# Three transformer layers on one core: x, the normalised x and the gated product at other SBUF addresses

## The chip, the core and the metric

The kernel runs on one core of a Trainium2 chip. The metric is the device time of one execution in microseconds (us), the median of the runs of a kernel. A profiled execution gives one trace: for every instruction its engine, start and length. PE is the matrix engine (TensorE), PEld its weight loads; DVE, ACT and POOL are the vector, scalar and GpSimd engines; SP only issues DMAs here.

## What is computed

Three layers over 256 tokens of width 1024, batch 1, float32 throughout: layer A (three dilated attentions of 16 heads), layer B (block attention of 16 heads) and layer C (attention of 8 heads with a forget gate, a convolution and a pooling branch), each followed by the same kind of gated MLP with a short causal convolution. Cut to the MLP, which the change names:

```python
def conv_ffn(h, w_up, conv_w, conv_b, w_down):
    u = h @ w_up                                     # 1024 -> 2 x 2816
    up = jnp.pad(u, ((0, 0), (CONV_WIDTH - 1, 0), (0, 0)))
    uc = conv_b + sum(conv_w[j] * up[:, j:j + S] for j in range(CONV_WIDTH))
    gate, val = uc[..., :D_FF], uc[..., D_FF:]
    return (jax.nn.silu(gate) * val) @ w_down        # 2816 -> 1024
```

## The kernel before

**Precision.** Every large product is made of three fp32r matmuls. A weight chunk arrives in `w_raw` by DMA; ACT copies it rounded into `w_hi` (L362), and DVE subtracts to get the rest, `w_lo` (L370). The activations are split alike: the normalised x into `xg` (for each of 8 blocks k of 128 channels, 256 tokens of the high part and then 256 of the low part), the attention's output into `mix_hi` and `mix_lo`, the MLP's gated product into `g_hi[b]` and `g_lo[b]` (two buffers each, b = 0, 1). hi·hi, hi·lo and lo·hi are summed in PSUM.

**Weight stream.** 372 chunks of up to 1024 columns pass through a ring of six buffers for each of `w_raw`, `w_hi` and `w_lo`. All waits are semaphores written by hand, and every engine runs its instructions in the order of the code.

**The stages on PE.** Each layer has

- attention (`unit_chunk_pe`): `xg` is the stationary operand (128 columns of a block), the weights move, 384 columns a matmul, lines L650, L651 and L652. The small matmuls of scores, transposes and values lie between them;
- the output projection (`out_pe`): a weight tile is stationary and `mix_hi` or `mix_lo` moves, 256 columns, lines L1189, L1190, L1191, eight times the three for a chunk;
- the MLP (`ffn_pe`), 24 steps j = 0 to 23. A step with j < 22 has two chunks of the up projection (`project2`): for each of eight blocks k one matmul of 512 columns, `w_hi` stationary and high and low part of `xg` moving (L402), then one of 256 columns, `w_lo` stationary and the high part moving (L404). A step with j > 1 then has one chunk of the down projection: for each of eight tiles m three matmuls of 256 columns, with a weight tile stationary and `g_hi[j % 2]` or `g_lo[j % 2]` moving (L1707, L1708, L1709). Steps 4 to 19 run in a loop of eight turns with two steps each. The up projection writes PSUM banks 0 and 1 in even steps, 2 and 3 in odd ones; the down projection adds into banks 4 to 7 throughout.

Layer C has six further chunks ahead of its attention (`project_k`, L388 to L390): weight stationary, `xg` moving, 256 columns, three matmuls for a block.

**Addresses.** SBUF tensors lie one behind the other in the order of the code, each on a multiple of 32 bytes. Addresses below are bytes within a partition; a float is 4 bytes, a 128-column slice 512 bytes, a 256-column one 1024. `x_all` holds 16 gains of the first norm in its first 64 bytes and x behind them (`xT`); `norm_gain` (called by ACT and DVE) reads the gains there for the first norm, and `load_x` on SP fills both.

Of the kernel before, what the change touches and what calls it, by code (L numbers as in the profile page):

```python
# [8 lines left out]
P = 128  # L9
D = 1024  # L10
TOK = 256
KT = D // P
# [27 lines left out]
WARM_UP = 16  # L40
HALVES = 3
GAINS = 16
CHUNK = KT * P
UNIT = 3 * P
QCHUNK = 2 * UNIT
# [112 lines left out]
def build(nc, x_d, xa_d, stream_d, par_d, con_d, taps_d, out_d):  # L158
# [7 lines left out]
    def sb(name, shape, dt=F32):  # L166
        return nc.alloc_sbuf_tensor(name, shape, dt)
# [5 lines left out]
    w_raw = [sb(f"w_raw{s}", [P, CHUNK]) for s in range(RING)]  # L173
    w_hi = [sb(f"w_hi{s}", [P, CHUNK], F32R) for s in range(RING)]
    w_lo = [sb(f"w_lo{s}", [P, CHUNK], F32R) for s in range(RING)]
    x_all = sb("x_all", [P, GAINS + KT * TOK])
    xT = x_all[:, GAINS:GAINS + KT * TOK].rearrange("p (k t) -> p k t", t=TOK)
    xg = sb("xg", [P, KT, 2, TOK], F32R)
    xg_hi, xg_lo = xg[:, :, 0, :], xg[:, :, 1, :]
    mix_hi = sb("mix_hi", [P, KT, TOK], F32R)  # L180
# [1 line left out]
    par = sb("par", [P, N_PAR])  # L182
    con = sb("con", [P, N_CON])
    zero = sb("zero", [P, TOK], BF16)
    ln_x = sb("ln_x", [P, TOK])
    rms_r = sb("rms_r", [P, TOK])

# [248 lines left out]
    def norm_gain(e, m):  # L436

        g = PAR_NORM + KT * e + m
        return x_all[:, m:m + 1] if e == 0 else par[:, g:g + 1]

    def first_hi_dve(eng):
        eng.wait_ge(x_first, 16)
# [1612 lines left out]
    with nc.Block() as block:  # L2055

        @block.sync
        def _(sp):
            def load(c):
                s, w = c % RING, chunk_cols(c)  # L2060
                sp.dma_start(w_raw[s][:, 0:w], stream_d[c, :, 0:w]).then_inc(w_loaded[s], 16)


            def load_half(c, kk):
                part = slice(kk * UNIT, (kk + 1) * UNIT)
                sp.dma_start(w_raw[c][:, part], stream_d[c, :, part]).then_inc(half_in[c] if kk == 0 else w_loaded[c], 16)

            def load_x(m, n, landed):
                part = slice(GAINS + m * TOK if m else 0, GAINS + (m + n) * TOK)
                sp.dma_start(x_all[:, part], xa_d[:, part]).then_inc(landed, 16)  # L2070

            load_x(0, 1, x_first)
            load_x(1, 1, x_in[0])
            for kk in range(2):
                load_half(1, kk)
            load_x(2, 2, x_in[1])
            for kk in range(2):
                load_half(2, kk)
            load(3)
            load_x(4, 2, x_in[2])  # L2080
            load(4)
            load(5)
            load_x(6, 2, x_in[3])
            sp.dma_start(con[:, 0:CON_MASKA], con_d[:, 0:CON_MASKA]).then_inc(con_in, 16)
            sp.dma_start(par[:, 0:PAR_FFN], par_d[:, 0:PAR_FFN]).then_inc(row_in, 16)
            for c in range(RING, N_CHUNKS):
                sp.wait_ge(w_lo_done, c - RING + 1)
                load(c)
                if c == RING + 10:
                    sp.dma_start(con[:, CON_MASKA:], con_d[:, CON_MASKA:]).then_inc(rest_in, 16)  # L2090
                if c == A_OUT:
                    sp.wait_ge(rest_in, 16)
                    sp.dma_start(par[:, PAR_FFN:], par_d[:, PAR_FFN:]).then_inc(rest_in, 16)
                if c == A_FFN:
                    sp.dma_start(taps[:], taps_d[:, :]).then_inc(taps_in, 16)
                if c == RING + 16:
                    sp.wait_ge(x_lo, KT)
                    sp.wait_ge(x_sq, KT)
                    for q in range(UCH):
                        sp.dma_start(xT[:, 2 * q:2 * q + 2], x_d[2 * q:2 * q + 2].rearrange("k p t -> p k t")).then_inc(x_in[q], 16)  # L2100
            for m in range(0, KT, 2):
                sp.wait_ge(x_new, 5 * KT + m + 1)
                sp.dma_start(out_d[m], xT[:, m, :]).then_inc(stored, 16)
            sp.wait_ge(stored, 16 * KT)

        @block.tensor
        def _(pe):

            pe.wait_ge(warm, 1)
            for n in range(WARM_UP):  # L2110
                nc.tensor.matmul(bank(7), zero[:, 0:P], zero[:], start=True, stop=True, skip_group_check=True)
            att_a_pe(pe)
            ffn_stage(pe, 0, ffn_pe(0))
            att_b_pe(pe)
            ffn_stage(pe, 1, ffn_pe(1))
            pre_pe(pe)
            att_c_pe(pe)
            ffn_stage(pe, 2, ffn_pe(2))

        @block.scalar  # L2120
        def _(act):
            for kk, landed in ((0, half_in[0]), (1, w_loaded[0])):
                part = slice(kk * UNIT, (kk + 1) * UNIT)
                act.dma_start(w_raw[0][:, part], stream_d[0, :, part]).then_inc(landed, 16)
            nc.scalar.preload_act_table_set("natural_log_exp_and_others")
            half_split_hi(act, 0, 0)
            half_split_hi(act, 0, 1)
            resid_act(act, 0, 1)
            half_split_hi(act, 1, 0)
            half_split_hi(act, 1, 1)  # L2130
            resid_act_sq(act, 0)
            resid_act_sq(act, 1)
            resid_act(act, 0, 2)
            half_split_hi(act, 2, 0)
            resid_act(act, 0, 3)
            half_split_hi(act, 2, 1)
            split_hi(act, 3)
            resid_act(act, 0, 4)
            resid_act(act, 0, 5)
            split_hi(act, 4)  # L2140
            split_hi(act, 5)
            resid_act(act, 0, 6)
            resid_act(act, 0, 7)
            resid_act_sq(act, 2)
            resid_act_sq(act, 3)
            att_a_act(act)
            ffn_stage(act, 0, ffn_act(0))
            nc.scalar.preload_act_table_set("natural_log_exp_and_others")
            end_act(act, 2)
            att_b_act(act)  # L2150
            ffn_stage(act, 1, ffn_act(1))
            nc.scalar.preload_act_table_set("natural_log_exp_and_others")
            end_act(act, 4)
            pre_act_f(act)
            att_c_act(act)
            ffn_stage(act, 2, ffn_act(2))
            for m in range(1, KT, 2):
                act.wait_ge(x_new, 5 * KT + m + 1)
                act.dma_start(out_d[m], xT[:, m, :]).then_inc(stored, 16)

        @block.vector
        def _(dve):
            nc.vector.memset(zero[:], 0.0).then_inc(warm, 1)
            first_hi_dve(dve)
            half_split_lo(dve, 0, 0)
            resid_dve_lo(dve, 0, 0)
            half_split_lo(dve, 0, 1)
            resid_dve_lo(dve, 0, 1)
            half_split_lo(dve, 1, 0)
            half_split_lo(dve, 1, 1)  # L2170
            resid_dve_lo(dve, 0, 2)
            half_split_lo(dve, 2, 0)
            resid_dve_lo(dve, 0, 3)
            half_split_lo(dve, 2, 1)
            split_lo(dve, 3)
            resid_dve_lo(dve, 0, 4)
            resid_dve_lo(dve, 0, 5)
            split_lo(dve, 4)
            split_lo(dve, 5)
            resid_dve_lo(dve, 0, 6)  # L2180
            resid_dve_lo(dve, 0, 7)
            gains_dve(dve)
            att_a_dve(dve)
            ffn_stage(dve, 0, ffn_dve(0))
            end_dve(dve, 2, acc, B_QKV)
            att_b_dve(dve)
            ffn_stage(dve, 1, ffn_dve(1))
            end_dve(dve, 4, acc, C_PRE)
            pre_dve_f(dve)
            att_c_dve(dve)  # L2190
            ffn_stage(dve, 2, ffn_dve(2))
            end_dve(dve, 6, acc, N_CHUNKS)

        @block.gpsimd
        def _(pool):
            nc.gpsimd.memset(cv_h[0][:], 0.0).then_inc(zeroed, 1)
            nc.gpsimd.memset(cv_h[1][:], 0.0).then_inc(zeroed, 1)
            resid_pool(pool, 0)
            tables_pool(pool)
            att_a_pool(pool)  # L2200
            resid_pool(pool, 1)
            ffn_stage(pool, 0, ffn_pool(0))
            resid_pool(pool, 2)
            att_b_pool(pool)
            resid_pool(pool, 3)
            ffn_stage(pool, 1, ffn_pool(1))
            resid_pool(pool, 4)
            pool_zeroes(pool)
            pre_pool_f(pool)
            resid_pool(pool, 5)  # L2210
            ffn_stage(pool, 2, ffn_pool(2))
# [62 lines left out]
def first_input(w):  # L2274

    x = np.zeros((P, GAINS + KT * TOK), np.float32)
    x[:, 0:KT] = w["attn_norm"][0].reshape(KT, P).T
    x[:, GAINS:] = w["x"][0].T[:, class_order()].reshape(KT, P, TOK).transpose(1, 0, 2).reshape(P, KT * TOK)
    return x
# [87 lines left out]
```

## Time and profile before

| | |
|---|---|
| median of 3 runs | 1060.22 us (1059.83 to 1062.07) |
| the profiled execution | 1060.19 us |
| its span, first to last instruction | 1058.4 us |
| PE busy | 1053.8 us, 7508 matmuls |
| PE weight loads busy | 981.7 us |
| DVE / ACT / POOL busy | 862.2 / 685.9 / 342.0 us |
| granted TensorE clock | 1.00 throughout |

The profile models the end of a matmul, and neighbours overlap in it: the length of one matmul (281 ns for 256 columns) isn't what it costs. The cost is the distance from its start to the next one's start. So the timeline is read here by starts: the start of a chunk's first matmul, subtracted from that of the next chunk.

### The profile page before, as it was taken

The page shows a single profiled execution, that of the slowest core. Times are in us where ns is not written, and L with a number is a line of the kernel's source. Part 1 is how long each engine was busy: PE and PEld are TensorE (multiplying, and loading weights), DVE is VectorE, ACT ScalarE, POOL GpSimd, SP SyncE. Part 2 cuts the span into 40 slices and gives each one's busy share as a digit, 9 for nine tenths or more (in the row PEclk, how much of TensorE's full clock was granted, in tenths as well). Part 3 has the DMA queues.
Part 4 walks back from the last instruction along what each step waited for, and adds up shares of the span by engine and source line. Part 5 has one row for each costly group of instructions (what it writes and reads, how often), then busy time and mean ns, then how long its engine had stood idle before and what let it go on. Part 6 is the DMA issues. An engine that isn't in the chain of part 4 may idle for free.

```text
span 1058.4 us, 21208 instructions
## 1 busy us (share of the span) xinstructions
PE 1053.8 (100%) x7508; PEld 981.7 (93%) x7508; DVE 862.2 (81%) x1588; ACT 685.9 (65%) x1262; POOL 342.0 (32%) x368
## 2 busy tenths in 40 slices
PE   9999999999999999999999999999999999999998
PEld 8999999999999999999989899999998999999998
DVE  7877778877799888887777998888896769988886
ACT  7766676776766555576776665555686666655552
POOL 4312222121365333322122553333350025533331
PEclk9999999999999999999999999999999999999999
DMA  9644545455466555535453675555434436655541
GB/s 317 225 159 150 164 151 180 149 185 196 161 219 198 195 181 190 159 110 179 152 164 120 216 216 187 188 187 189 134 112 144 146 114 225 212 187 190 183 154 41
DMA packets 57749, 183.34 MB, mean 173 GB/s; under 512 B 6352, under 2 KB 9680, under 8 KB 57424
## 3 DMA queue, kind: packets, MB, share of 16 engines
q1 hardware_dynamic: 56816, 181.52, 52.7%
q8 instruction: 41, 0.67, 0.3%
q10 hardware_dynamic: 864, 0.92, 0.3%
q14 instruction: 28, 0.23, 0.1%
HBM read 181.36 MB, written 1.05 MB: 172 GB/s over the span
## 4 chain that ended last, share of the span: by engine, by line
PE 99%; DMA 0%; DVE 0%; ACT 0%; DVEq 0%; issue 0%
PE ps L402 23%; PE ps L404 12%; PE ps L650 10%; PE ps L652 9%; PE ps L651 9%; PE ps L1707 6%; PE ps L1709 6%; PE ps L1708 6%; PE ps L1189 2%; PE ps L1191 2%; PE ps L1190 2%; PE ps L584 1%; PE ps L809 1%; PE ps L854 1%; PE ps L783 1%; PE ps L821 1%
## 5 line engine op out<-in xcount | busy, mean ns | idle before, releaser
L370 DVE TENSOR_TENSOR w_lo<-w_raw,w_hi 128x1024 fp32r<-128x1024 f32 (+2 forms) x369 | 441.0, 1210 | 56.0 <-ACT w_hi L362 55.3
L362 ACT ACTIVATE w_hi<-w_raw 128x1024 fp32r<-128x1024 f32 (+2 forms) x369 | 354.1, 972 | 163.3 <-PE ps L404 136.6
L402 PE MATMUL ps<-xg,w_hi 128*128 128x512 f32 x1056 | 374.7, 396 | 0.0
L404 PE MATMUL ps<-xg,w_lo 128*128 128x256 f32 x1056 | 297.0, 281 | 0.0
L402 PEld LDWEIGHTS ps<-xg,w_hi 128*128 128x128 f32 x1056 | 198.6, 188 | 44.6
L404 PEld LDWEIGHTS ps<-xg,w_lo 128*128 128x128 f32 x1056 | 198.1, 188 | 0.1
L1829 POOL TENSOR_TENSOR prob_t<-prob_t,qkT 128x256 f32<-128x256 f32 x63 | 100.3, 1593 | 289.6 <-ACT prob_t L1752 289.6
L650 PE MATMUL ps<-w_hi,xg 128*128 128x384 f32 (+1 forms) x556 | 193.1, 347 | 0.0
L652 PE MATMUL ps<-w_hi,xg 128*128 128x384 f32 (+1 forms) x556 | 186.8, 336 | 0.0
L651 PE MATMUL ps<-w_lo,xg 128*128 128x384 f32 (+1 forms) x556 | 186.7, 336 | 0.0
L1707 PE MATMUL ps<-g_hi,w_hi 128*128 128x256 f32 x528 | 149.2, 283 | 0.0
L1709 PE MATMUL ps<-g_hi,w_lo 128*128 128x256 f32 x528 | 148.9, 282 | 0.0
L1708 PE MATMUL ps<-g_lo,w_hi 128*128 128x256 f32 x528 | 148.6, 281 | 0.0
L1823 POOL TENSOR_TENSOR qkT<-prob,rms_r 128x256 f32<-128x256 f32 x132 | 119.2, 922 | 19.0 <-DVE prob L1766 10.3
L1799 DVE SCALAR_TENSOR_TENSOR qkT<-qkT,par 128x255 f32<-128x255 f32 (+1 forms) x264 | 111.6, 476 | 4.3 <-ACT qkT L1745 4.2
L650 PEld LDWEIGHTS ps<-w_hi,xg 128*128 128x128 f32 x556 | 104.4, 188 | 3.4 <-issue 2.7
L651 PEld LDWEIGHTS ps<-w_lo,xg 128*128 128x128 f32 x556 | 104.5, 188 | 0.1
L652 PEld LDWEIGHTS ps<-w_hi,xg 128*128 128x128 f32 x556 | 104.3, 188 | 0.0
L1707 PEld LDWEIGHTS ps<-g_hi,w_hi 128*128 128x128 f32 x528 | 99.6, 189 | 2.7
L1745 ACT ACTIVATE qkT<-qkT,par 128x256 f32<-128x256 f32 x132 | 76.4, 597 | 37.6 <-POOL qkT L1823 37.4
L1708 PEld LDWEIGHTS ps<-g_lo,w_hi 128*128 128x128 f32 x528 | 99.7, 189 | 0.0
L1709 PEld LDWEIGHTS ps<-g_hi,w_lo 128*128 128x128 f32 x528 | 99.3, 188 | 0.0
(182 smaller groups left out, 1388.5 us busy)
## 6 DMA issues: line engine op xcount, KB each, us to landing
w_raw<-w_stream SPq DMA_DIRECT2D x228, 512.0 KB, 3.6
w_raw<-w_stream SPq DMA_DIRECT2D x137, 384.0 KB, 3.4
w_raw<-w_stream SPq DMA_DIRECT2D x4, 392.0 KB, 3.0
con<-consts SPq DMA_DIRECT2D x1, 1024.0 KB, 7.5
x_all<-x_t SPq DMA_DIRECT2D x4, 256.0 KB, 5.5
conv_taps<-taps SPq DMA_DIRECT2D x1, 1024.0 KB, 7.1
w_raw<-w_stream SPq DMA_DIRECT2D x4, 192.0 KB, 4.4
x_all<-x_a SPq DMA_DIRECT2D x3, 256.0 KB, 5.5
```

What stands on the lines that cost most here:

```text
L362: nc.scalar.activation(w_hi[s][:, 0:w], w_raw[s][:, 0:w], ACT.Copy).then_inc(w_hi_done, 1)
L370: nc.vector.tensor_tensor(w_lo[s][:, 0:w], w_raw[s][:, 0:w], w_hi[s][:, 0:w].bitcast(F32), ALU.subtract).then_inc(w_lo_done, 1)
L402: nc.tensor.matmul(bank(b, 0, 2 * TOK), w_hi[s][:, k * P:(k + 1) * P], xg[:, k, :, :].rearrange("p h t -> p (h t)"), start=(k == 0), stop= ...
L404: last = nc.tensor.matmul(bank(b), w_lo[s][:, k * P:(k + 1) * P], xg_hi[:, k, :], start=False, stop=(k == KT - 1), skip_group_check=True)
L650: nc.tensor.matmul(out, hi, wh, start=(k == 0), stop=False)
L651: nc.tensor.matmul(out, hi, wl, start=False, stop=False)
L652: last = nc.tensor.matmul(out, lo, wh, start=False, stop=(k == KT - 1))
L1707: nc.tensor.matmul(acc(m), wh, g_hi[b][:], start=first, stop=False, skip_group_check=True)
L1708: nc.tensor.matmul(acc(m), wh, g_lo[b][:], start=False, stop=False, skip_group_check=True)
L1709: last = nc.tensor.matmul(acc(m), wl, g_hi[b][:], start=False, stop=True, skip_group_check=True)
L1799: nc.vector.scalar_tensor_tensor(cv_s[b][s][:, k:TOK], up_s[b][s][:, 0:TOK - k], par_col(f, t, per, i, 4 * s + 2 - k), cv_s[b][s][:, k:TOK ...
L1823: nc.gpsimd.tensor_tensor(up_s[t % 2][s], up_sum[s], rms_r[:], ALU.mult).then_inc(F.up, 1)
```

## The change

Only where tensors lie in SBUF changes. `X0` = 256 floats now stand ahead of x in `x_all`, and the gains occupy the last 16 of them; so x's split between gains and data falls 1024 bytes into `x_all` in place of 64 bytes. An unused tensor `gap` of 176 floats is put behind `zero`. Instructions, their order on every engine, their waits and the sizes of the transfers stay as they are.

| tensor | address before, modulo 1024 (128) | after, modulo 1024 (128) |
|---|---|---|
| w_raw, w_hi, w_lo, slice k | 128 + 512k (0) | the same |
| x (`xT`) | 192 (64) | 128 (0) |
| xg, high and low part of each block | 192 (64) | 128 (0) |
| mix_hi, mix_lo | 192 (64) | 128 (0) |
| con | 64 (64) | 0 (0) |
| ln_x, rms_r, tokbuf, qkT, v_tok, prob0, prob_t | 96 (96) | 736 (96) |
| g_hi, g_lo, both buffers | 256 (0) | 896 (0) |

```diff
+X0 = TOK
+GAP = 176
...
-    x_all = sb("x_all", [P, GAINS + KT * TOK])
-    xT = x_all[:, GAINS:GAINS + KT * TOK].rearrange("p (k t) -> p k t", t=TOK)
+    x_all = sb("x_all", [P, X0 + KT * TOK])
+    xT = x_all[:, X0:X0 + KT * TOK].rearrange("p (k t) -> p k t", t=TOK)
...
     zero = sb("zero", [P, TOK], BF16)
+    sb("gap", [P, GAP])
     ln_x = sb("ln_x", [P, TOK])
...
-        return x_all[:, m:m + 1] if e == 0 else par[:, g:g + 1]
+        return x_all[:, X0 - GAINS + m:X0 - GAINS + m + 1] if e == 0 else par[:, g:g + 1]
...
-                part = slice(GAINS + m * TOK if m else 0, GAINS + (m + n) * TOK)
-                sp.dma_start(x_all[:, part], xa_d[:, part]).then_inc(landed, 16)
+                a, b = GAINS + m * TOK if m else 0, GAINS + (m + n) * TOK
+                sp.dma_start(x_all[:, X0 - GAINS + a:X0 - GAINS + b], xa_d[:, a:b]).then_inc(landed, 16)
```

## Rows read from the trace of the kernel before

**Rows 1.** The page: span, engines' busy us, the granted TensorE clock.
```profile
span 1058.4 us, 21208 instructions
PE 1053.8 (100%) x7508; PEld 981.7 (93%) x7508; DVE 862.2 (81%) x1588; ACT 685.9 (65%) x1262; POOL 342.0 (32%) x368
PEclk9999999999999999999999999999999999999999
```
**Rows 2.** The page's chain that ended last, shares of the span.
```profile
PE 99%; DMA 0%; DVE 0%; ACT 0%; DVEq 0%; issue 0%
```
**Rows 3.** Waits of PE: waiter <- releaser: us in total, times, longest.
```profile
PE ps L2111 <- DVE zero L2163: 1.1, 1, 1.1
PE ps L584 <- ACT w_hi L377: 0.4, 1, 0.4
```
**Rows 4.** Matmuls by line: names, array, shape, count | busy us, mean ns | idle before.
```profile
L402 PE MATMUL ps<-xg,w_hi 128*128 128x512 f32 x1056 | 374.7, 396 | 0.0
L404 PE MATMUL ps<-xg,w_lo 128*128 128x256 f32 x1056 | 297.0, 281 | 0.0
L650 PE MATMUL ps<-w_hi,xg 128*128 128x384 f32 x540 | 187.5, 347 | 0.0
L1707 PE MATMUL ps<-g_hi,w_hi 128*128 128x256 f32 x528 | 149.2, 283 | 0.0
L1189 PE MATMUL ps<-mix_hi,w_hi 128*128 128x256 f32 x192 | 55.5, 289 | 0.0
```
**Rows 5.** Timeline, layer A's MLP: first matmuls of chunks (start us, us, matmul).
```profile
347.58 0.40 PE L402 MATMUL ps<-xg,w_hi 128*128 128x512 f32 x1
...
353.17 0.28 PE L1707 MATMUL ps<-g_hi,w_hi 128*128 128x256 f32 x1
...
356.01 0.40 PE L402 MATMUL ps<-xg,w_hi 128*128 128x512 f32 x1
...
361.67 0.28 PE L1707 MATMUL ps<-g_hi,w_hi 128*128 128x256 f32 x1
...
364.55 0.40 PE L402 MATMUL ps<-xg,w_hi 128*128 128x512 f32 x1
```
**Rows 6.** Timeline, layer B's output projection: first matmuls, 24 apart in each pair.
```profile
564.17 0.28 PE L1189 MATMUL ps<-mix_hi,w_hi 128*128 128x256 f32 x1
...
566.89 0.28 PE L1189 MATMUL ps<-mix_hi,w_hi 128*128 128x256 f32 x1
...
573.13 0.28 PE L1189 MATMUL ps<-mix_hi,w_hi 128*128 128x256 f32 x1
...
575.96 0.28 PE L1189 MATMUL ps<-mix_hi,w_hi 128*128 128x256 f32 x1
```
**Rows 7.** Timeline, attention: starts 12 matmuls apart, in layers A and B.
```profile
43.38 0.34 PE L650 MATMUL ps<-w_hi,xg 128*128 128x384 f32 x1
...
45.45 0.34 PE L650 MATMUL ps<-w_hi,xg 128*128 128x384 f32 x1
...
476.59 0.34 PE L650 MATMUL ps<-w_hi,xg 128*128 128x384 f32 x1
...
478.71 0.34 PE L650 MATMUL ps<-w_hi,xg 128*128 128x384 f32 x1
```
**Rows 8.** Timeline, layer B's first MLP chunk, and the next two pairs behind.
```profile
577.37 0.39 PE L402 MATMUL ps<-xg,w_hi 128*128 128x512 f32 x1
...
580.16 0.40 PE L402 MATMUL ps<-xg,w_hi 128*128 128x512 f32 x1
...
581.21 0.47 PE L402 MATMUL ps<-xg,w_hi 128*128 128x512 f32 x1
581.52 0.28 PE L404 MATMUL ps<-xg,w_lo 128*128 128x256 f32 x1
```
**Rows 9.** The page: groups of DVE and ACT, and a DMA issue.
```profile
L370 DVE TENSOR_TENSOR w_lo<-w_raw,w_hi 128x1024 fp32r<-128x1024 f32 (+2 forms) x369 | 441.0, 1210 | 56.0 <-ACT w_hi L362 55.3
x_all<-x_a SPq DMA_DIRECT2D x3, 256.0 KB, 5.5
```

## The prediction

> **What bounds the kernel now.** I read the page first. PE is busy for 1053.8 of 1058.4 us and the clock is granted in full in every slice [rows 1]; the chain that ended last is 99% PE [rows 2]; and PE's waits on other engines sum to 1.5 us, all at the start [rows 3]. DVE, ACT and POOL have room: DVE's largest group alone sits idle for 56.0 us, mostly waiting for ACT, which itself works ahead of PE [rows 9]. So the time is a sum over 7508 matmuls of the distance from one start to the next, and the change can matter only through these distances.
>
> They aren't N columns divided by 2.4 GHz. The timeline gives them: in layer A's MLP two up chunks (16 pairs of L402 and L404) take 353.17 - 347.58 = 5.59 us and the next two 361.67 - 356.01 = 5.66; one down chunk (24 matmuls of 256 columns) takes 2.84 us from 353.17 and the next 2.88 us from 361.67 [rows 5]. At 2.4 GHz 24 x 256 columns alone would be 2.56 us. So each chunk carries 9 to 12% that no wait accounts for, and the amount has two values for the same instructions. The timeline repeats this in all three MLPs: of 132 up chunks 62 go at half of 5.59 and 70 at half of 5.66; of 66 down chunks the 30 of the even steps up to j = 20 take 2.88 and the other 36 take 2.84 to 2.85.
>
> Two more rows say what kind of thing this is. The output projection has the same instructions as the down projection, with `mix` moving in place of `g`: its 24 matmuls take 2.72 us at one place and 2.83 at another [rows 6]. Attention's twelve matmuls of 384 columns take 2.07 us, or 2.12 [rows 7]. A pattern holds until something disturbs it: layer B's first MLP chunk goes at 2.79 us for eight pairs, has a hitch (0.31 us from an L402 to its L404, about 0.08 more than elsewhere) [rows 8], and goes in the slower pattern behind it. The pace is a state of PE's two operand streams, the weight loads and the moving reads, which lock to one another; addresses could have a part in which locks there are.
>
> **The change, part by part.**
>
> *Work and order.* Nothing is added or removed: the rows of PE, DVE, ACT, POOL and SP are the same in the same order with the same waits. Cost 0.
>
> *Other engines.* `w_raw`, `w_hi` and `w_lo` stay where they are, so the 441.0 us of DVE's split [rows 9] keep their addresses. What moves is x, xg, the attention's buffers and g. If these instructions got slower, PE's cover is the weight ring: it has waited for nobody since the start [rows 3]. x's first transfers land on other addresses, 64 bytes further within 128. That is ahead of the first matmul; the three large ones take 5.5 us to land [rows 9] for the same bytes. I take 0, with 0.1 us either way.
>
> *The down projection* (L1707 to L1709, 1584 matmuls; one line's 528 in [rows 4]). `g` goes from 256 to 896 modulo 1024, on a multiple of 128 both times. Here only the distance to the stationary weights changes: they start at 128 or 640, so g starts 128 behind one of them before and 256 behind one after. Bounds, from the nearest rows with these instructions: 2.72 us a chunk below [rows 6], 2.88 above [rows 5]. I take 2.83, the commoner pattern of the output projection, since the long runs of chunks there keep to it. The sum: 30 x (2.88 - 2.83) = 1.5, and 36 x 0.01 = 0.4: **-1.9 us**. The bounds are 30 x 0.16 + 36 x 0.12 = 9.1 us less, and 36 x 0.035 = 1.3 us more.
>
> *The up projection* (L402, L404, 1056 each [rows 4]). `xg` moves from 64 past a multiple of 128 onto one, and its distance to the weights falls from 64 to 0. The trace shows two patterns that take turns with the down projection's: a 2.88 chunk is followed by fast up chunks, a 2.84 chunk by slow ones [rows 5]. If the down projection settles in one pattern, the turns should end. The steps would then all be fast (70 chunks x 0.035 = 2.45 us less) or all slow (62 x 0.035 = 2.2 us more). I take fast, **-2.45 us**: after the 2.83 pattern of the output projection, layer B's MLP began with 2.79 for eight pairs, which is the fast one [rows 8]. The step leans on one place and is the weakest of the sum.
>
> *Attention and output projection.* `xg` is stationary there and moves by the same 64 bytes; the moving weights stay. 92 of 139 twelves are in the 2.07 pattern, the rest higher. All of them at 2.12 would be 92 x 0.05 = 4.6 us more, all at 2.07 some 2 us less. I see no reason for either and take 0.
>
> The sum is -1.9 - 2.45 = -4.35 us. The profiled execution took 1060.19 us, the median is 1060.22, so both give **1055.8 us**.
>
> **What the skill says.** The trace shows a cost that isn't in the column count (2.84 against 2.56 us [rows 5]) and differs for the same instruction. The Trainium skill, TensorE: Matmul & The Clock Gate, Step-by-step, says that PE has two independent SBUF read ports, so that loading the next weights takes nothing from the running matmul; its section Back-to-back issue gap has N/2.4 + 2.5 ns. By that 24 matmuls of 256 columns would take about 2.62 us (an estimate from that page), wherever they lie. The trace doesn't bear the figure out, in any pattern. SBUF — State Buffer of the same skill, Specifications, has cachelines of 16 bytes; all operands start on one before and after. By both pages the change would do nothing, which is the first rival.
>
> **The rivals.**
>
> 1. *Addresses of this kind don't matter.* Both patterns occur in one stage with the same addresses (up chunks at 5.59 and 5.66 [rows 5]), so what chooses between them is history, and the new addresses only redraw it to the same mix. For it: `xg`, off 128, and `g`, on 128, differ by little. Time: 1060.2. Chance 0.20.
> 2. *A deeper lock.* The new distances let the MLP lock where the output projection did for some chunks. The down chunks at 2.72 are 9.1 us less; the up projection at the rate per column of attention's 2.07 (2.07 / 12 / 384 = 0.449 ns) takes 16 x 768 x 0.449 ns = 5.52 us in place of a mean of 5.625, times 66 steps 6.9 us less: 1044.2, or 1051 if it is the down projection alone. Against it: no MLP chunk of the trace shows that lock. Chance 0.14.
> 3. *Slower: what lies on 128 goes slowest.* Of the moving operands of 256 columns the one on a multiple of 128, `g`, is the slowest in the trace (2.84 to 2.88), and `mix`, 64 off, is faster (2.72 to 2.83) [rows 5, 6]. If that is due to the multiple of 128, `xg` joins it. The place is the up projection. With every MLP chunk in the slower of its own two patterns the price is 2.2 + 1.3 = 3.5 us, 1063.7. At g's rate per column (2.88 / 24 / 256 = 0.469 ns) a step's 16 pairs would take 5.76 us, up to 8.9 us more. It decides as soon as more than half of the up steps fall into the slow pattern with nothing gained in the down projection. Against it: moving weights lie on 128 too, and attention has a good pattern with them (2.07 [rows 7]). Chance 0.28.
>
> **How the numbers follow.** The forecast, 1055.8, has 0.38; the deeper lock 0.14; nothing 0.20; slower 0.28. A measurement of this kernel can tell about 0.2%, 2.1 us, from no change: faster 0.38 + 0.14 = 0.52, the same 0.20, slower 0.28. The range reaches from the full deeper lock, 1044, past rival 3's price with part of attention's 4.6 us, to 1065. About 0.04 lie below and 0.09 above. Cases of both signs hold most of it; the forecast's own range is 1053 to 1058 (one of its two terms missing, or part of the deeper lock).
>
> **What would show it.** In the trace after, down chunks of 24 matmuls at 2.83 us or under, where 2.88 and 2.84 took turns; pairs of up chunks at 5.59 without turns; attention's twelves at 2.07 as before; PE still waiting for nobody. Down chunks still at 2.84 to 2.88 refute the first term, up chunks at 5.66 the second. If all starts are spaced as before, rival 1 holds; if starts are unchanged and the time isn't, then something outside PE's streams (a wait, a transfer at the start) does it, and the whole reading is wrong.

## The result

The changed kernel takes 1063.44 us (median of 19 runs, 1063.17 to 1063.70), the kernel before 1060.08 us on the same chip: a ratio of 1.0025, 95% interval 1.0018 to 1.0033. It is slower, by 3.4 us, where 4.4 us less were forecast.

The page of the changed kernel, span, busy times and clock, to be held against [rows 1]:

```profile
span 1061.7 us, 21208 instructions
PE 1056.7 (100%) x7508; PEld 982.6 (93%) x7508; DVE 862.1 (81%) x1588; ACT 685.8 (65%) x1262; POOL 339.0 (32%) x368
PEclk9999999999999999999999999999999999999999
```

Its chain and PE's waits (as [rows 2, 3]):

```profile
PE 97%; DVE 1%; DMA 1%; SPq 1%; ACT 0%; POOL 0%; issue 0%; DVEq 0%; POOLq 0%
```
```profile
PE ps L2114 <- DVE zero L2166: 1.1, 1, 1.1
PE ps L587 <- ACT w_hi L380: 0.5, 1, 0.5
PE ps L700 <- POOL tokbuf L1162: 0.3, 1, 0.3
```

PE waits for others for 1.9 us in place of 1.5, at full clock. The rest of the 3.3 us of span is in the distances from one matmul's start to the next. The timeline of layer A's MLP after the change, first matmuls of chunks, answers to [rows 5] (lines are 3 further down in the file: L1710 was L1707, L405 was L402, L1192 was L1189):

```profile
353.77 0.28 PE L1710 MATMUL ps<-g_hi,w_hi 128*128 128x256 f32 x1
...
356.64 0.40 PE L405 MATMUL ps<-xg,w_hi 128*128 128x512 f32 x1
...
362.29 0.28 PE L1710 MATMUL ps<-g_hi,w_hi 128*128 128x256 f32 x1
...
365.18 0.40 PE L405 MATMUL ps<-xg,w_hi 128*128 128x512 f32 x1
```

Down chunks take 2.87 and 2.89 us; they took 2.84 and 2.88. A pair of up chunks takes 5.65, and from step 3 on every such pair does, where 5.59 and 5.66 took turns. And the output projection of layer B, 24 matmuls from start to start, where [rows 6] had 2.72 and 2.83:

```profile
573.12 0.28 PE L1192 MATMUL ps<-mix_hi,w_hi 128*128 128x256 f32 x1
...
576.00 0.28 PE L1192 MATMUL ps<-mix_hi,w_hi 128*128 128x256 f32 x1
```

2.88 us, that is 120.0 ns a matmul.

The table below is what all experiments are read by. It sums, over a whole trace, the distance from each matmul's start to the next one's, by the stage of the first. "D" is the distance in bytes from the start of the stationary weight tile to the start of the moving operand, modulo 512 (a tile is 512 bytes wide, so every tile of a chunk looks the same); the changed kernel's g starts 768 bytes behind the weights' start, so its D is 256. In attention the roles are turned, xg being the stationary operand; it is listed under the same D of xg. A chunk's ns a matmul, or a pair, is its time to the next chunk's start divided by its 24 matmuls, or its 8 pairs.

| kernel | D of xg, mix, g | median us | attention | output proj. | up | down |
|---|---|---|---|---|---|---|
| before | 64, 64, 128 | 1060.1 | 298.7 | 70.0 | 372.1 | 188.5 |
| changed | 0, 0, 256 | 1063.4 | 298.9 | 71.4 | 372.8 | 189.9 |
| e1_x_only | 0, 0, 128 | 1061.8 | 298.7 | 71.4 | 372.7 | 188.1 |
| e2_g_only | 64, 64, 256 | 1058.3 | 301.1 | 70.1 | 370.0 | 189.0 |
| e3_g_64 | 64, 64, 192 | 1057.4 | 301.2 | 70.1 | 373.9 | 179.9 |
| e4_all_64_on | 0, 0, 256 | 1063.5 | 298.5 | 71.4 | 372.8 | 189.9 |
| e5_all_192 | 192, 192, 192 | 1057.0 | 297.7 | 68.8 | 373.8 | 186.4 |
| e6_g_320_448 | 64, 64, 320 and 448 | 1058.4 | 298.6 | 70.0 | 373.6 | 184.8 |
| e7_g_64_96 | 64, 64, 64 and 96 | 1061.2 | 298.7 | 70.0 | 373.7 | 187.9 |
| e8_x_448_g_192 | 448, 448, 192 | 1057.0 | 298.0 | 68.8 | 373.8 | 186.4 |
| e9_x_192_g_64 | 192, 192, 64 | 1056.5 | 298.0 | 68.8 | 373.0 | 186.5 |
| e10_weights_alone | 0, 0, 64 | 1055.6 | 298.7 | 71.4 | 369.5 | 185.8 |
| e11_x_320_g_448 | 320, 320, 448 | 1056.0 | 298.7 | 70.0 | 373.6 | 182.0 |
| e12_x_0_mix_192_g_192 | 0, 192, 192 | 1047.0 | 298.1 | 68.8 | 368.3 | 180.9 |
| e13_x_0_mix_192_g_64 | 0, 192, 64 | 1052.7 | 297.6 | 68.8 | 369.8 | 185.6 |
| e14_gap_32 | 0, 0, 192 | 1049.7 | 299.4 | 71.4 | 367.8 | 180.8 |

Attention has two values where xg is at D = 64. In the trace of the kernel before most twelves of layer A are at 2.07 us; in those of e2_g_only and e3_g_64, with the same addresses there, most are near 2.12 (176.5 ns a matmul). Layer A's attention takes 196.0 us in the first and 198.5 in the other two; layers B and C differ by 0.1 at most. That fits the runs of the kernel before, which lie in two groups, near 1060.0 and 1062.2. The profiled execution of e2_g_only had the dearer attention and lies above the median (1061.12 against 1058.33 us). That of e3_g_64 had it too, and is still the fastest of its seven (1055.94, median 1057.35), so its other executions lost more in some other stage: one trace isn't the median in every stage. The other stages are compared from the traces, the whole by medians and intervals.

### The profile page after: what moved, and what is told of

It reads as the page before. It is cut to its first block, busy times and chain, and to the rows that moved or that the text cites. A ratio compares the mean times of both kernels' runs of the same rounds, so it can differ in the third digit from the quotient of the medians.

```text
span 1061.7 us, 21208 instructions
## 1 busy us (share of the span) xinstructions
PE 1056.7 (100%) x7508; PEld 982.6 (93%) x7508; DVE 862.1 (81%) x1588; ACT 685.8 (65%) x1262; POOL 339.0 (32%) x368
## 4 chain that ended last, share of the span: by engine, by line
PE 97%; DVE 1%; DMA 1%; SPq 1%; ACT 0%; POOL 0%; issue 0%; DVEq 0%; POOLq 0%
PE ps L405 23%; PE ps L407 12%; PE ps L653 9%; PE ps L655 9%; PE ps L654 9%; PE ps L1712 6%; PE ps L1711 6%; PE ps L1710 6%; PE ps L1192 2%; PE ps L1193 2%; PE ps L1194 2%; PE ps L812 1%; PE ps L857 1%; PE ps L786 1%; PE ps L824 1%; PE ps L843 1%
## 5 line engine op out<-in xcount | busy, mean ns | idle before, releaser
L405 PE MATMUL ps<-xg,w_hi 128*128 128x512 f32 x1056 | 375.5, 398 | 0.0
L405 PEld LDWEIGHTS ps<-xg,w_hi 128*128 128x128 f32 x1056 | 198.5, 188 | 46.0
L655 PE MATMUL ps<-w_hi,xg 128*128 128x384 f32 (+1 forms) x556 | 186.5, 336 | 0.0
L1710 PE MATMUL ps<-g_hi,w_hi 128*128 128x256 f32 x528 | 149.4, 283 | 0.0
L1826 POOL TENSOR_TENSOR qkT<-prob,rms_r 128x256 f32<-128x256 f32 x132 | 116.3, 899 | 19.2 <-ACT rms_r L518 7.0
L1710 PEld LDWEIGHTS ps<-g_hi,w_hi 128*128 128x128 f32 x528 | 100.3, 190 | 2.9
```

Source lines behind the costliest of these rows:

```text
L405: nc.tensor.matmul(bank(b, 0, 2 * TOK), w_hi[s][:, k * P:(k + 1) * P], xg[:, k, :, :].rearrange("p h t -> p (h t)"), start=(k == 0), stop= ...
L655: last = nc.tensor.matmul(out, lo, wh, start=False, stop=(k == KT - 1))
L1710: nc.tensor.matmul(acc(m), wh, g_hi[b][:], start=first, stop=False, skip_group_check=True)
L1826: nc.gpsimd.tensor_tensor(up_s[t % 2][s], up_sum[s], rms_r[:], ALU.mult).then_inc(F.up, 1)
```

## The experiments

The first question was which of the moved things costs the time, and whether a tile's own address or its distance to the weights does it.

**x alone, g alone.**

```diff
# e1_x_only: the change's lines for x with X0 = 256, and
+    sb("gap", [P, 16])
# e2_g_only: only, ahead of g_hi,
+    sb("gap_g", [P, 160])
```

> x, xg, mix and con move as in the change (xg and mix from 192 to 128 modulo 1024); an unused 16 floats behind zero bring everything from ln_x to g back to its residue of before (g at 256). Theory 1 (what counts is where the moving operand starts modulo 128: at 0 a matmul of 256 columns goes at 120 ns, at 64 at 113 to 118): the output projection at 120.0 ns, no up chunk pattern of before; g was on 128 already, so almost the whole +0.25% is here, 1062.6 to 1063.6. Theory 2 (the distance modulo 1024 to the weights, xg's and g's each on its own): part of it only, with the down projection as before (turns of 2.88 and 2.84 us a chunk). Theory 3 (the tail from 96 to 736, that is the buffers of DVE and ACT, costs the time): 1060.

> Only g (and the convolution's buffers behind it) moves by 640 bytes, to 896 modulo 1024; x, xg, mix and the rest as before. Theory 1: g is on a multiple of 128 both times, so 1060.1 within 0.1%, down chunks 2.84 to 2.88 us. Theory 2: the distance of g to the weights counts, and the down chunks change, 1 to 2 us either way.

x alone: 1061.79 us, ratio 1.0013 (1.0004 to 1.0022). The output projection goes to 71.4 us and most of its matmuls to 120.0 ns, as theory 1 had it; the sum of the down projection stays (188.1), though its turns of 2.88 and 2.84 end and nearly all its chunks go at 118.5 ns a matmul. That theory's price for the whole, +0.25%, was too high. g alone: 1058.33 us, 0.9983 (0.9974 to 0.9992), a gain. The down chunks get 0.6 us dearer, but up chunks, whose operands haven't moved, get 2.1 us cheaper: 116 of 132 at 349 to 350 ns a pair. So g's address acts on the up projection as well; that it does so through the pattern in which a down chunk hands over is my reading, not shown. The two parts sum to -0.2 us where the change has +3.4: with xg at 0 the up chunks lose what g at 256 gives them at 64. Theory 3 (buffers of DVE and ACT) doesn't explain e1, which leaves them at their residues. Neither run moves them from 96 to 736, as the change does; but DVE and ACT are as busy after it as before (862.1 and 685.8 us) and PE waits for others 0.4 us more in all, and what the change has over e1 lies in the down projection (189.9 against 188.1), whose operand g is.

**g at 64 past a multiple of 128.** `gap_g` of 16 floats, nothing else.

> The kernel before with g moved by 64 bytes, to 320 modulo 1024 and 64 past a multiple of 128, as xg and mix are. Theory 1: the down chunks take the output projection's patterns of before, 2.83 us or 2.72, which is 1.9 to 9.1 us less: 1051 to 1058. Theory 2 (distance 192 to the weights, which occurs nowhere yet): no forecast, 1058 to 1062. If 64 past 128 has no part in it: 1060.

1057.35 us, 0.9972 (0.9961 to 0.9983). The timeline, as [rows 5]:

```profile
346.29 0.28 PE L1708 MATMUL ps<-g_hi,w_hi 128*128 128x256 f32 x1
...
349.01 0.40 PE L403 MATMUL ps<-xg,w_hi 128*128 128x512 f32 x1
...
354.67 0.28 PE L1708 MATMUL ps<-g_hi,w_hi 128*128 128x256 f32 x1
```

The down chunk takes 2.72 us, the lower bound of the prediction, and 64 of 66 chunks do, within 0.03: 8.5 us less in this trace for 64 bytes. The up pairs are all slow now (5.66), which gives 1.9 us back.

**Place or distance?** Two runs. In the first every tensor is 64 bytes further, with all distances as in the changed kernel; in the second only the weights' 18 buffers are moved by 64 bytes; x, xg, mix, con, g and the tail (the buffers from `ln_x` on) lie 1024 bytes further and so keep their residues modulo 1024 of before.

```diff
# e4_all_64_on: the changed kernel, and ahead of w_raw
+    sb("gap_w", [P, 16])
# e10_weights_alone: the kernel before with X0 = 256, no gap, and ahead of w_raw
+    sb("gap_w", [P, 16])
```

> The changed kernel with 16 unused floats ahead of all tensors: weights, xg, mix and g all lie 64 bytes further, all 64 past a multiple of 128, with the distances between them as in the changed kernel. If the distance between moving and stationary operand counts: as the changed kernel, 1063.4, output projection at 120.0 ns a matmul. If the moving operand's own place modulo 128 counts (theory 1): output projection at 113 to 118 ns, down chunks 2.72 to 2.83 us, 1052 to 1058.

> Only the weights' buffers move, by 64 bytes; x, xg, mix, con, the tail and g keep their residues modulo 1024 of before. So a moving operand that lay 64 behind the weights' start now lies at 0, and g, which lay 128 behind, at 64. If a tile's own place sets its pace: as before in every stage, 1060.1. If its distance to the stationary operand does: output projection at 120.0 ns a matmul (71.4 us in place of 70.0) as in the changed kernel though mix hasn't moved, up pairs of 346 and 353 ns, and down chunks at 2.83 us or 2.72 as at D = 64: 1053 to 1061.

The first is the changed kernel again: 1063.54 us, and up (372.8) and down (189.9) agree with it to the tenth. Its output projection:

```profile
573.14 0.28 PE L1192 MATMUL ps<-mix_hi,w_hi 128*128 128x256 f32 x1
...
576.02 0.28 PE L1192 MATMUL ps<-mix_hi,w_hi 128*128 128x256 f32 x1
```

2.88 us, though mix lies 64 past a multiple of 128 here, as it did at 2.72 and 2.83. In the second, mix has its residue of before, and the weights have not; the timeline of its output projection and of its MLP:

```profile
571.66 0.28 PE L1191 MATMUL ps<-mix_hi,w_hi 128*128 128x256 f32 x1
...
574.54 0.28 PE L1191 MATMUL ps<-mix_hi,w_hi 128*128 128x256 f32 x1
```
```profile
352.74 0.28 PE L1709 MATMUL ps<-g_hi,w_hi 128*128 128x256 f32 x1
...
355.57 0.40 PE L404 MATMUL ps<-xg,w_hi 128*128 128x512 f32 x1
...
361.12 0.28 PE L1709 MATMUL ps<-g_hi,w_hi 128*128 128x256 f32 x1
```

2.88 us again with mix at its residue of before, a down chunk at 2.83, a pair of up chunks at 5.55 (84 of the 132 up chunks are at 347 to 348 ns a pair, most others at 352 to 354), and 1055.57 us in all, 0.9951 (0.9937 to 0.9965). This settles it: what counts is the distance between the tile that is being loaded and the one that moves. A tile's own place, and the multiple of 128 by itself, count for nothing that these runs show. The Trainium skill, TensorE: Matmul & The Clock Gate, Step-by-step, says that loading the next weights doesn't steal read bandwidth from the running matmul; here moving the weights alone by 64 bytes changed the spacing of matmuls whose moving operand kept its residue, from 117.8 or 113.3 to 120.0 ns. No run here shows how many ports there are or what the two reads share; that the spacing doesn't depend on where the load reads isn't so in this stream.

**Which distances?** With g in both buffers, or xg and mix, at other D:

```diff
# e5_all_192: X0 = 48, gap of 224, gap_g of 16;  e8_x_448_g_192: X0 = 112, gap of 160, gap_g of 16
# e6_g_320_448, e7_g_64_96: g_hi0, g_lo0, a gap, then g_hi1, g_lo1, so that even
# and odd steps have their own D; the gaps are 48 and 32 floats in e6, 240 and 8 in e7
```

> What is left after the first four: the distance from the weights' start to the moving operand's, D. So far, 256 columns a matmul: D = 0 (mix) 120.0 ns; 64 (mix) 117.8, at times 113.3; 128 (g) 118.3 to 120; 192 (g) 113.3 in 64 of 66 chunks; 768 (g) 119.5 to 120. Here everything moving in MLP and output projection lies at D = 192, the tail's residues as before. If D alone sets the pace: output projection 113.3 ns throughout (2.5 us less), down chunks 2.72 us, up pairs under the 349 ns of before (a bound is 113 + 229 = 342, 1056 pairs, 7 us less); attention, where xg is stationary and D has its sign turned, unknown, up to 5 us more. Sum 1043 to 1054. If g's gain has to do with g alone: output projection at 117.8, 1054 to 1058.

> As the run with everything at 192, but xg and mix at D = 448 and g at 192. With a period of 256 in D it is the same as that run in every stage. With a period of 512 up chunks, attention and output projection may differ from it, down chunks not. 1043 to 1058.

e5: 1057.02 us (0.9970, 0.9958 to 0.9982), e8: 1057.01. They are one kernel in every stage of the table, to 0.3 us in attention and 0.1 elsewhere; so for xg and mix a step of 256 bytes changes nothing. The output projection fell by 1.2 us, not by the 2.5 forecast, and my bound for the up pairs (342 ns) was wishful: 126 of 132 chunks sit at 352 to 354, the others higher. The down chunks disappointed most: g is at D = 192 as in e3_g_64, yet takes 2.82 us:

```profile
351.98 0.28 PE L1710 MATMUL ps<-g_hi,w_hi 128*128 128x256 f32 x1
...
354.80 0.40 PE L405 MATMUL ps<-xg,w_hi 128*128 128x512 f32 x1
...
360.46 0.28 PE L1710 MATMUL ps<-g_hi,w_hi 128*128 128x256 f32 x1
```

So one D allows several patterns, and what runs ahead of the chunk appears to pick one of them.

> The kernel before with g's two buffers at different D: even steps 320, odd steps 448 (modulo 512 the weights look the same for every tile). If the period in D is 128: both at 113.3 ns as D = 192 is. If it is 256: 320 goes as 64 does (117.8), 448 as 192 does (113.3). If it is 512: neither is known. 1051 to 1060.

> The kernel before with g in even steps at D = 64 and in odd steps at D = 96. If D alone sets the pace, 64 goes as the output projection of before (117.8 ns, at times 113.3), whatever tile it is; 96 is off every multiple of 64: no forecast, between 113.3 and 120. 1053 to 1060.

e6: 1058.38 us, 0.9986 (0.9977 to 0.9996). 49 of its 66 down chunks are at 117.7 to 118.0 ns a matmul and 17 at about 113.5, all of these in odd steps, D = 448, and not all odd steps. e7: 1061.16 us, 1.0008 (0.9998 to 1.0017), no clear change: its even steps (D = 64) go at 117.8, two chunks aside, its odd ones (96) at 119.6 to 120.1. In no trace did a down chunk go at 113.3 with D a multiple of 128, and in none did it settle at 119 or more with D an odd multiple of 64: eight such chunks in e10 and e12 to e14 have a mean of 121, all by a first distance of 0.19 us, with 118 ns behind it.

```diff
# e9_x_192_g_64: X0 = 48, gap of 224, gap_g of 240
# e11_x_320_g_448: X0 = 80, gap of 192, gap_g of 80
```

> xg and mix at D = 192 behind the weights' start, where attention kept its good pattern in every run (297.7 to 298.0 us in place of 298.7 or 301.2), and g at D = 64. If the down projection's pattern goes by how g lies to xg (128 apart in the run with down chunks of 2.72 us, 0 apart in the one with 2.83), it is 128 apart here too: down chunks 2.72 us, output projection 68.8 us, 1052 to 1054. If it goes by g's own D (192 good, 64 not): down chunks 2.83, 1057.

> xg and mix at D = 320, g at 448: the run with xg at 64 and g at 192, both 256 bytes further. With a period of 256 in D it is that run again: down chunks 2.72 us (179.9 in all), up pairs 353 ns, output projection 70.0 us, 1056 to 1059 by attention's pattern. If the period is 512 or more, some stage differs.

e9: 1056.45 us, 0.9958 (0.9945 to 0.9972), down 186.5: that g is 128 from xg isn't what gave e3 its down chunks. e11: 1056.00 us, 0.9958 (0.9943 to 0.9973): up and output projection are e3's, the down chunks aren't quite (43 at 113.5 and 22 at 117.8, where e3 has 64 at 113.5). Whether a period of 256 holds for g strictly is open; the slower executions of e3 may have such chunks too, and one trace of each doesn't tell.

**Putting it together.** What stayed open was the change itself: is xg at D = 0 bad, or only in the company of that g?

```diff
# e12_x_0_mix_192_g_192: X0 = 256, gap of 224, gap_g of 16, and ahead of mix_hi
+    sb("gap_mix", [P, 48])
# e13_x_0_mix_192_g_64: the same with gap_g of 240
```

> xg at D = 0 as in the changed kernel, mix on its own at 192, g at 192. If each moving operand sets its own stage by its D and the up projection's pattern goes by which g runs between its chunks: output projection 68.8 us (not 71.4), down chunks 113.3 or 117.8 ns a matmul (180 to 187 us in all), up pairs at 346 ns if g at 192 does as g at 64 did (369.5 us in all), 353 if not (373). 1048 to 1057.

> As the last one with g at D = 64: the distances of the run in which the weights alone moved, made by moving the activations instead, and mix at 192. If distances are all that counts: that run's MLP (555.2 us in all, up pairs mostly 346 ns) with the output projection 2.6 us shorter, 1053.0. If it isn't that run less 2.6 us, mix's pattern carries over into the MLP, or something beside distances counts.

e13: 1052.69 us, 0.9923 (0.9908 to 0.9937), forecast 1053.0: e10's MLP with e5's output projection. e12: 1046.95 us, 0.9869 (0.9852 to 0.9886), below its range and the fastest of all. Its MLP:

```profile
353.87 0.39 PE L406 MATMUL ps<-xg,w_hi 128*128 128x512 f32 x1
...
359.42 0.28 PE L1711 MATMUL ps<-g_hi,w_hi 128*128 128x256 f32 x1
...
362.15 0.39 PE L406 MATMUL ps<-xg,w_hi 128*128 128x512 f32 x1
```

5.55 us for a pair of up chunks and 2.73 for a down chunk, both without turns (118 of 132 up chunks at 347 ns a pair, 58 of 66 down chunks at 113.5 a matmul). So xg at D = 0, with g at 192, is the best place for the up projection that was tried, and the change had put xg there.

Last, in the changed kernel one number:

```diff
-GAP = 176
+GAP = 32
```

> The changed kernel with one number of it changed: the unused floats are 32 in place of 176, so g lies at D = 192 and not at 768; x, xg and mix stay at D = 0 as changed, the tail moves with g. If g's distance is what spoiled the changed kernel's MLP: up pairs 347 ns (368.3 us in all, not 372.8), down chunks mostly 113.3 ns a matmul (181 us, not 190), output projection at 120 as changed (71.4): 1049.5 us, 1.3% under the changed kernel. If the last gain (1046.95) rested on mix or on the tail's residues: above 1055.

```profile
356.05 0.39 PE L405 MATMUL ps<-xg,w_hi 128*128 128x512 f32 x1
...
361.60 0.28 PE L1710 MATMUL ps<-g_hi,w_hi 128*128 128x256 f32 x1
...
364.33 0.39 PE L405 MATMUL ps<-xg,w_hi 128*128 128x512 f32 x1
```

1049.74 us against 1060.00 for the kernel before, 0.9900 (0.9883 to 0.9916); forecast 1049.5. Moving g, and with it the buffers behind `zero`, by 576 bytes back (g from 896 to 320 modulo 1024) makes 13.7 us of difference to the changed kernel; in the traces 9.1 are in the down projection and 5.0 in the up projection. The tail lies at 160 here and at 96 in e12, and the two agree in both to 0.5 us.

The trace of e12 still has PE waiting for nobody to speak of, though each layer has a stop of 0.15 to 0.3 us ahead of the down chunk of step 3, which the list doesn't show and no run explains:

```profile
PE ps L2115 <- DVE zero L2167: 1.1, 1, 1.1
PE ps L588 <- ACT w_hi L381: 0.6, 1, 0.6
PE ps L701 <- POOL tokbuf L1163: 0.3, 1, 0.3
```

## Why the prediction was wrong

*What bounds the kernel* held: PE's start-to-start distances, and nothing else, carried the change; the other engines' moved buffers cost nothing that shows. The reading that the pace is a state of the two operand streams in which addresses have a part fits all runs. The terms of the sum, in size and sign, did not hold:

- *Down projection*, forecast -1.9 us, measured 189.94 - 188.46 = **+1.5**. This is the step that failed first: "I take 2.83, the commoner pattern of the output projection". The nearest row was chosen by the likeness of the instructions. By distance the output projection was at 64 and the new g at 256, while g's own chunks, 2.84 to 2.88 at 128, were rows at a multiple of 128 like it. The nearer row was the upper bound, and the measured +1.5 lies just past the +1.3 given for it.
- *Up projection*, forecast -2.45, measured **+0.7**. "If the down projection settles in one pattern, the turns should end": they ended, in the slow one. "I take fast" failed. It leaned on layer B's first MLP chunk behind the output projection's 2.83 pattern, and layer A, in the same trace and behind the same pattern, began in the slow one, 279.23 - 276.41 = 2.82 us:

```profile
276.41 0.40 PE L402 MATMUL ps<-xg,w_hi 128*128 128x512 f32 x1
...
279.23 0.40 PE L402 MATMUL ps<-xg,w_hi 128*128 128x512 f32 x1
```

  After the change, outside steps 1 and 2 all 120 chunks are at 352 to 354 ns a pair, and steps 3 to 21 cost 1.4 us more than before, where +2.2 was given as the other end. The 12 chunks of steps 1 and 2, which have no down chunk among them, went at 346 (a first distance of 0.42 us aside) and gave 0.6 back. This 346 was visible in no row before, and e12 shows it for the whole stage.
- *Output projection*, taken as 0, measured **+1.3**. It was lumped with attention, where xg is stationary; but in the output projection mix moves, and went to the same D = 0. The term was put at nothing by a wrong reading of who moves.
- *Attention*, taken as 0, measured +0.2; the chunks ahead of layer C's attention +0.1; the first 14 us -0.7.

The four stages and these ends make the 3.3 us of span to within 0.2.

*The figure of the Trainium skill.* The prediction sets 2.62 us a chunk, worked out with N/2.4 + 2.5 ns, against the trace. The same section of the Trainium skill, TensorE: Matmul & The Clock Gate, Back-to-back issue gap, calls that formula the gap of an isolated matmul and not that of a stream with a weight load each; so that no pattern here meets it, the best being 2.72, says less than the prediction makes of it.

*The rivals.* Rival 3 named the right rows and the right time (1063.7 against 1063.44) for a reason that is wrong as stated: a multiple of 128 in a tile's own address does no harm (e4 has all tiles off it and the same time, and e12 has its fastest stage with xg on it). It holds only because the weights lie on one too, so that the distance becomes one. That the time fits to 0.3 us is luck: its price was 2.2 us in the up and 1.3 in the down projection, and measured were 0.7 and 1.5, with 1.3 in the output projection, which it didn't have. Rival 1, addresses don't matter, is refuted by e10. Rival 2, the deeper lock, was real at 2.72 us a down chunk, within 0.01 of its bound (e3, e12, e14), but the change didn't reach it.

*The range* held the time; the forecast's own range (1053 to 1058) did not.

## What to carry to other kernels

In a kernel bound by back-to-back fp32r matmuls with a weight load each, subtract starts in the timeline and compare the same instruction between stages before touching anything: here the same 256 columns took 113.3, 117.8 or 120.0 ns and the same pair 346 to 354, and addresses alone were worth 1.3% of the whole (1059.96 to 1046.95 us). Choose the distance modulo 512 between the tile that is loaded and the tile that moves, not each tile's alignment, and choose it stage by stage: of the distances tried, an odd multiple of 64 did best for 256 columns and 0 for the mixed stream of 512 and 256 columns, provided that the stage between its chunks had its own good distance. To price such a change, take the row with the same distance, not only the same instruction; where no row has that distance, as for g at 256 here, measure before you sum.

## What the runs showed of the hardware

That the relative address of two reads of one engine matters was the surprise: e4 moves both and nothing changes, e10 moves one and the spacing does. Three further points. The patterns are exact and repeat over hundreds of microseconds, and after a hitch or a change of stage another one can hold: the down projection at D = 192 ran at 113.5 in most chunks behind up chunks of xg at D = 64 or 0 (e3, e12, e14), and at 117.8 behind those at 192 or 448 (e5, e8). Attention with xg at D = 64 had one of two patterns (298.7 or 301.2 us) in traces with the same addresses in that stage; at D = 192 or 448 the traces had only the cheaper one (297.7 and 298.0), and the runs of e5 and e8 lie within 0.4 and 0.2 us in place of 3. What in the memory makes two streams collide at some distances wasn't measured; that both read the same part of it at the same time is a guess which fits, and no more.
